# Turnovers between sublayers of a two-layer trunk: sums as 32-column strips partly ahead of the last weight half, low parts of h on GpSimd, and a new order of the first projections

## The reference

```python
def pre_norm(x, mod, j, g):
    return rmsnorm(x, g) * (1 + mod_chunk(mod, 3 * j + 1)) + mod_chunk(mod, 3 * j)

def post_residual(x, out, mod, j, g, w):
    return x + w * mod_chunk(mod, 3 * j + 2) * rmsnorm(out, g)

def swiglu(h, w_in, w_out):
    gate, up = jnp.split(h @ w_in, 2, axis=-1)
    return (jax.nn.silu(gate) * up) @ w_out
```

## Time and profile before

| | |
|---|---|
| median of 3 runs | 1605.79 us (1604.51 to 1605.99) |
| the profiled execution | 1602.07 us |
| its span | 1600.1 us |
| busy, share of the span | PE 96%, DVE 68%, ACT 43%, POOL 3% |
| chain that ended last | PE 81%, DVE 10%, ACT 3% |
| TensorE clock granted | full over the whole span |
| data moved | 259.77 MB, mean 162 GB/s |

### The profile page before, as it was taken

One profiled execution on the slowest core, in us unless ns is written; L12 is line 12 of the kernel. 1 busy time (PEld: TensorE's weight loads), 2 busy tenths in 40 slices (PEclk: granted clock), 3 DMA queues, 4 the chain that ended last, 5 costly groups with the idle time before them and its releaser, 6 DMA issues.

```text
span 1600.1 us, 26085 instructions
## 1 busy us (share of the span) xinstructions
PE 1541.0 (96%) x10631; PEld 1505.8 (94%) x10631; DVE 1085.4 (68%) x1975; ACT 691.0 (43%) x1204; POOL 50.3 (3%) x50
## 2 busy tenths in 40 slices
PE   4999999999889899999999999999999999999999
PEld 4999999989778889999999999999999989999999
DVE  5678889773579797878946778785562885344332
ACT  4433334464566474333434533334463265333333
POOL 2000000002102000000000000000000000000000
PEclk9999999999999999999999999999999999999999
DMA  9765656577321264564545555655454354443311
GB/s 325 249 201 168 200 181 223 184 223 213 89 92 56 66 211 158 185 206 160 197 157 184 167 193 184 197 176 173 133 192 132 106 176 141 131 132 124 102 64 39
DMA packets 255654, 259.77 MB, mean 162 GB/s; under 512 B 6625, under 2 KB 253842, under 8 KB 255538
## 3 DMA queue, kind: packets, MB, share of 16 engines
q1 hardware_dynamic: 250528, 253.25, 48.8%
q10 hardware_dynamic: 4114, 2.84, 0.6%
q0 software_dynamic: 896, 2.06, 0.5%
HBM read 255.50 MB, written 2.62 MB: 161 GB/s over the span
## 4 chain that ended last, share of the span: by engine, by line
PE 81%; DVE 10%; ACT 3%; issue 3%; POOL 1%; DMA 1%; ACTq 0%; DVEq 0%; POOLq 0%
PE bank L444 24%; PE bank L446 24%; PE bank L445 24%; DVE PARTS L1112 1%; DVE WL L413 1%; ACT WH L399 1%; PE bank L466 1%; PE bank L1638 1%; PE bank L468 1%; PE bank L467 1%; DVE X L1178 1%; DVE HL L1141 1%; DVE SUMS L1443 1%; POOL WL L413 1%; DMA MIX<-in_x_sample 1%
## 5 line engine op out<-in xcount | busy, mean ns | idle before, releaser
L413 DVE TENSOR_TENSOR WL<-RAW,WH 128x1024 fp32r<-128x1024 f32 (+1 forms) x335 | 398.6, 1195 | 418.5 <-ACT WH L399 417.7
L399 ACT ACTIVATE WH<-RAW 128x1024 fp32r<-128x1024 f32 (+1 forms) x344 | 357.5, 1043 | 605.3 <-PE bank L446 593.1
L444 PE MATMUL bank<-HH,WH 128*128 128x384 f32 x1664 | 564.2, 339 | 8.0 <-DVE WL L413 3.5
L446 PE MATMUL bank<-HH,WL 128*128 128x384 f32 x1664 | 560.6, 337 | 0.0
L445 PE MATMUL bank<-HL,WH 128*128 128x384 f32 x1664 | 560.4, 337 | 0.0
L444 PEld LDWEIGHTS bank<-HH,WH 128*128 128x128 f32 x1664 | 313.8, 189 | 10.0 <-issue 4.0
L445 PEld LDWEIGHTS bank<-HL,WH 128*128 128x128 f32 x1664 | 313.8, 189 | 0.0
L446 PEld LDWEIGHTS bank<-HH,WL 128*128 128x128 f32 x1664 | 313.7, 189 | 0.0
L444 PE MATMUL bank<-AH,WH 128*128 128x384 f32 x704 | 237.0, 337 | 0.0
L445 PE MATMUL bank<-AL,WH 128*128 128x384 f32 x704 | 236.6, 336 | 0.0
L446 PE MATMUL bank<-AH,WL 128*128 128x384 f32 x704 | 236.6, 336 | 0.0
(11 more groups left out here) (249 smaller groups left out, 1457.2 us busy)
## 6 DMA issues: line engine op xcount, KB each, us to landing
RAW<-in_ffn_w_in SPq DMA_DIRECT2D x88, 1024.0 KB, 5.1
RAW<-in_mod_w SPq DMA_DIRECT2D x72, 1024.0 KB, 5.1
RAW<-in_ffn_w_out SPq DMA_DIRECT2D x32, 1024.0 KB, 5.1
RAW<-in_ab_w_in SPq DMA_DIRECT2D x16, 1024.0 KB, 6.1
RAW<-in_ffn_w_out SPq DMA_DIRECT2D x16, 768.0 KB, 4.6
RAW<-in_cv_w_in SPq DMA_DIRECT2D x12, 1024.0 KB, 5.2
RAW<-in_ab_w_out SPq DMA_DIRECT2D x4, 1024.0 KB, 5.2
RAW<-in_cv_w_out SPq DMA_DIRECT2D x4, 1024.0 KB, 5.2
```

The lines of the kernel that those rows point to most:

```text
L399: e.activation(WH[:, (2 * m + b) % 4, 0:nk, :], RAW[:, p, 0:nk, b * P:(b + 1) * P], ACT.Copy).then_inc(half_hi, 1)
L413: e.tensor_tensor(WL[:, k, 0:nk, :], RAW[:, p, 0:nk, b * P:(b + 1) * P], WH[:, k, 0:nk, :].bitcast(F32), ALU.subtract).then_inc(half_ready, 1)
L444: e.matmul(out, WH[:, k, kk, :], xh(kk), start=(first and kk == 0), stop=False)
L446: mm = e.matmul(out, WL[:, k, kk, :], xh(kk), start=False, stop=(last and kk == nk - 1))
```

## The change

Six edits go together.

1. **Sums as strips.** Each sum matmul of 128 token columns becomes four matmuls of 32 columns, each into its own 32 partitions of the bank. `SUM_COLS` goes from 44 to 16.
2. **Part of the sums ahead.** The sums of the tiles 0 to 5 run ahead of the last output weight half (`early_sums`). Tiles 6 and 7 are no longer added to them by DVE but enter as sums of their own with weights `W67`. DVE's adds go from 24 to 20 a turnover and ACT squares one tile less.
3. **Operands in PSUM.** The small steps of DVE keep `q` in bank 2, `scale_y` writes into bank 3 (tile 0) or bank 7 and waits for all eight scaled tiles from tile 1 on. `spread` uses transposes in place of matmuls.
4. **h.** `HL` of tiles 1 to 7 is made by GpSimd (`low_parts`). The full copy of tiles 3, 5 and 7 is made by DVE, of the others by ACT. DVE makes the sample columns of `HH` of tile 0 itself.
5. **`pe_four`** does both products with `HH` of a tile for all four banks first and then the ones with `HL`; its tail is two tiles long from sublayer 1 on.
6. **Filler steps** are dealt out anew, and ACT does the root ahead of a weight split.

The core of the diff:

```diff
-SUM_COLS = 44
+SUM_COLS = 16
+FULL_DVE = (3, 5, 7)
...
-            high_ready(order[0])
...
-            for kk in order[1:len(order) - tail]:
-                ready(kk)
-                for b in range(4):
-                    e.matmul(outs[b], WH[:, kh[b], kk, :], HH[:, kk, :], start=False, stop=False)
-                    e.matmul(outs[b], WH[:, kh[b], kk, :], HL[:, kk, :], start=False, stop=False)
-                    e.matmul(outs[b], WL[:, kh[b], kk, :], HH[:, kk, :], start=False, stop=False)
-                yield
+            for kk in order[:len(order) - tail]:
+                first = kk == order[0]
+                high_ready(kk)
+                for b in range(4):
+                    if first:
+                        e.wait_ge(half_hi, H + b + 1)
+                    e.matmul(outs[b], WH[:, kh[b], kk, :], HH[:, kk, :], start=first, stop=False)
+                for b in range(4):
+                    if first:
+                        e.wait_ge(half_ready, H + b + 1)
+                    e.matmul(outs[b], WL[:, kh[b], kk, :], HH[:, kk, :], start=False, stop=False)
+                if first:
+                    yield
+                ready(kk)
+                for b in range(4):
+                    e.matmul(outs[b], WH[:, kh[b], kk, :], HL[:, kk, :], start=False, stop=False)
+                yield
...
+            def low_parts(s):
+
+                for d in range(1, KD):
+                    pool.wait_ge(*full_done(s, d))
+                    pool.wait_ge(h_hi, 8 * s + d + 1)
+                    pool.wait_ge(h_ready, 8 * s + d)
+                    pool.tensor_tensor(HL[:, d, :], TT[:, 2 + d % 2, :], HH[:, d, :].bitcast(F32),
+                                       ALU.subtract).then_inc(h_ready, 1)
...
                 root(sum_out(bank[0], 0), 0, (stat_done, 2 * s + 1))
+                nxt[1]()
+                root(STAT[:, 4, :], 5, (sum_step, 5 * (s + 1)))
                 act.wait_ge(xy_done, 8 * s + 8)
                 tile_scaled(s, OUT, 7)
-                root(STAT[:, 4, :], 5, (sum_step, 5 * (s + 1)))
...
-                dve.tensor_tensor(OUT[:, d, :], OUT[:, d, :], cols3(bank[4]), ALU.mult).then_inc(y_scaled, 1)
+                dve.tensor_tensor(scaled_y(OUT, d), OUT[:, d, :], cols3(bank[4]), ALU.mult).then_inc(y_scaled, 1)
...
-                full(s, 0)
+                dve.wait_ge(h_scaled, 8 * s + 1)
+                dve.tensor_scalar(HH[:, 0, SEQ:NT], TT[:, 0, SEQ:NT], CA[:, s, 0, 1:2], MOD[:, 24 * s, 1:2],
+                                  ALU.mult, ALU.add).then_inc(h_hi_sample, 1)
...
-                    low(s, d - 1)
                     if d == 1:
+                        low(s, 0)
+                    if d in FULL_DVE:
                         full(s, d)
-                low(s, KD - 1)
...
-                    mm = pe.matmul(B[:, columns(t)], src[:, t * P:(t + 1) * P], weights(t),
-                                   start=opens and t == 0, stop=closes and t == TOKS - 1)
+                    for strip in range(4):
+                        at = 32 * strip
+                        mm = pe.matmul(B[at:at + 32, columns(t)], src[:, t * P + at:t * P + at + 32], weights(t),
+                                       start=opens and t == 0, stop=closes and t == TOKS - 1)
...
+            def early_sums(s):
+
+                pe.wait_ge(sq_added, 5 * s + 5)
+                sums(bank[0], ACC, one, lambda t: sum_at(t, 0), opens=True)
+                pe.wait_ge(y_added, 5 * s + 5)
+                sums(bank[0], RSTD, one, lambda t: sum_at(t, 1))
+                pe.wait_ge(xy_added, 5 * s + 5)
+                sums(bank[1], ROOT, one, lambda t: sum_at(t, 0), opens=True)
...
+                            if j == 11 and b == 1 and s in SUMMED:
+                                early_sums(s)
...
+                        if d == 7:
+                            early_sums(s)
                         pe_half(pe, f"out{s}", d, hh, hl, 8, cols3(bank[4 + d % 4]), True, True)
```

More of the change, by code:

```diff
@@ L416, in split_dve, with full_done @@
             return out
+        def full_done(s, d):
+            if s == 0:
+                return h_full_dve, d + 1
+            if d in FULL_DVE:
+                return h_full_dve, KD + len(FULL_DVE) * (s - 1) + FULL_DVE.index(d) + 1
+            rest = [k for k in range(KD) if k not in FULL_DVE]
+            return h_full_act, len(rest) * (s - 1) + rest.index(d) + 1
         def out_nk(st, n):
@@ L647, in _ @@
                 half_low(f"in{s}")
+                low_parts(s)
         @block.scalar
```

139 lines of the change are left out of this document (74 added, 65 removed).

## The result

The changed kernel takes 1616.11 us (median of 4 runs, 1612.41 to 1616.84), the kernel before 1605.15 (4 runs beside them): a ratio of 1.0066, interval [1.0051, 1.0082]. It is slower, and outside the forecast range. The profiled execution took 1616.84 us, span 1615.0, mean granted clock of TensorE 0.986; before it was 0.996 and a span of 1600.1. So the clock wasn't full over the whole span before the change either, as the table ahead has it: it stood at 1.2 GHz in the opening (about 24 to 30 us) and for 3.4 us each at 426 and 463 us. Nor is that profile a typical execution: over the 72 executions of the kernel before that ran beside the experiments the mean granted clock runs from 0.990 to 0.996 (median 0.993) and the time from 1600.28 to 1607.42 us, and only ten of them reach 0.995.

What follows compares the result with a forecast made beforehand. TensorE, busy 96% of the span, was taken as the bound. SwiGLU turnovers -5.1, sublayers 1 and 4 +1.5 and last turnover -0.4 sum to -4.0 us: 1601.8 against the median of 1605.79, range 1593.5 to 1608.

Steps and rivals of the forecast that it cites:

- The strip's price: Sums in the turnovers: a unit of four strip matmuls costs 0.09 us, where a full matmul costs 0.236.
- rival 3: Strips load one after another, a unit at 0.236 us; 1615.4 us; chance 0.06.
- The wait of sublayers 1 and 4: Ahead of their last output tile, TensorE waits for DVE's adds of tile 5, idle for 4.1 us.
- T' to the first wide matmul: SwiGLU turnovers: last tile's end, delayed 0.97 us by early sums, to first wide matmul with h: 6.39 us.
- Last turnover: End of the kernel: strips let the root start at 1592.35, not at 1592.78; 0.4 us off.
- GpSimd's low part: h stage: one low part of a tile made by GpSimd takes 0.95 us.
- the last tile ends 4.54 later: Sublayers 1 and 4: waiting for DVE's adds delays the last tile's end 4.54 us; turnovers lose 0.76 and 0.75.
- First wide to next: ... waits 1.7, sum 19.54: From first wide matmul with h to the first projection behind the first four: 19.54 us, waits 1.7 included.
- three `full` of 0.6: h stage: DVE's full copies of tiles 3, 5, 7 take 0.6 us each; last `scaled` 14.5 after the first.
- rival 2: GpSimd becomes the bound of h, DVE and GpSimd holding each other up; 1614.3 us at low parts of 2.0; chance 0.13.
- the opening: Start of the kernel: keeps a tail of one and its wait for GpSimd's four weight halves; no gain.
- Rival 4: Turnovers not shortened, only the idle 1.2 and 0.8 behind the first four gained; 1605.3 us; chance 0.18.

Runs made afterwards that it cites:

- the fastest kernel: Changed kernel with a tail of one; in sublayers 1 and 4 three filler steps, then early sums as whole matmuls, behind the last tile: 1599.06 us, 0.9963.
- three runs: Changed kernel, early sums of sublayers 1 and 4 behind last tile: alone 1614.43 us; with tail of one and filler ahead 1605.51 or behind 1604.63.

## Why the prediction was wrong

**What held.** The strip's price: 72 records of the early sums take 0.80 us, 0.09 a unit, as taken; here the row was right and rival 3 fell. (By the rule of the Trainium skill that the prediction weighed, "TensorE: Matmul & The Clock Gate", section "LDWEIGHTS (loading the stationary operand)", the unit would have stayed at 0.236; the measurement decides against it.) The spread: 0.54 us for three transposes, as taken. The wait of sublayers 1 and 4: with no wait the last tile of sublayer 1 would have begun at 570.54, and it began at 575.12, 4.58 later against 4.54 forecast; 3.21 of it was idle, where I had 4.1. (That 575.12 is also near my 575.4 is luck: the stretch ahead of it was 1.1 us longer than in the profile of before, and began 1.4 earlier.) T' to the first wide matmul: 6.39 forecast, 6.41 in sublayer 0 and 6.03 and 6.04 in 1 and 4. No idle stands behind the first four any more, as forecast. Last turnover: 0.36 off, 0.4 forecast. GpSimd's low part: 0.99 to 1.03 us, 0.95 forecast.

**Failed: "the last tile ends 4.54 later" and every other term that counts standing at its own length.** The sum priced idle time at what it lasts, and so had sublayers 1 and 4 lose 0.76 and 0.75; they lost 5.79 and 5.75. Here idle time also brought TensorE from 2.4 to 1.2 GHz, for 3.4 or 6.8 us: the last tile started 4.58 later and ended 7.3 later. That was readable before: it lost 6.8 us of clock in all, with a fall in the opening, and I didn't ask where new idle of 4 us would leave the clock. The wait alone on the kernel before gives 10.4 us in the medians, where standing alone accounts for 7.2 (twice 4.04, less the 0.44 that each turnover gives back) and the clock behind the two waits for 5.1 in its profile; dummy work in the same wait gives back 5.5.

**Failed: "First wide to next: ... waits 1.7, sum 19.54".** It is 21.28, 21.10 and 21.11 where the clock held (sublayers 0, 1, 4). Beside 16.66 for the matmuls, 0.57 for filler and 0.36 for the modulation transpose, 3.7 remain in sublayer 0, where the sum had 1.9. Of these, 2.06 are named waits, where I had 1.7, and 1.6 are pauses of up to 0.2 us at each halt and each change between groups of matmuls, where I had 0.2; the kernel before has 0.9 of them. The waits go back to "three `full` of 0.6": each pair takes 1.43 to 1.48 beside GpSimd, and the last `scaled` comes 15.53 behind the first, not 14.5. That is rival 2's mechanism, in `full` rather than in the low parts. In exchange for the 1.22 us behind the first four, the tail of two waits 1.14 for the high part of tile 7 and 0.63 for its low part, and behind those the clock fell in two of five turnovers. A tail of one gives 21.09 to 20.43 without a fall there: the second tile held back is worth nothing in the first turnover (0.2) and costs 0.7 to 2.2 in the others. I had seen the 0.65 for the high part and had not seen that the tail makes it longer.

**Left out: that many small instructions in one go stall.** A strip costs 0.011 us a record, but there are four matmuls for one. The changed kernel itself has the stall in sublayer 2:

```profile
871.80 0.33 PE L1679 MATMUL bank<-W,SQ 128*32 128x32 f32 x14 [1.10 <-issue]
```

and one of 0.86 in sublayer 3. With them T to first wide is 7.43 and 7.28 us there and 6.41 in sublayer 0 (0.23 of "issue"). Neither the kernel before nor the one with strips in their old place shows one.

**Left out: the opening.** I gave it nothing; it gained 1.26. The new `pe_four` alone gains 0.96 there, strips and transposes alone 0.41. With the high products first, TensorE has eight matmuls of a tile to do before it asks for the low part; that this is where the 0.96 comes from isn't shown.

**The sum again.** Forecast -4.0 for the span. Take the clock's 15.4 off the measured 14.9, and -0.5 is left; in the medians, 8.4 off 11.0, +2.6 is left. With their 1.7 of clock off, the stretches to next of sublayers 0, 2 and 3 gained 0.1 and lost 1.0 and 0.7. Rival 4 had the turnovers no shorter, but with 1.0 gained in each of these, so it comes nearest and is still too good. Rival 2's 1614.3 comes near the measured time by accident: its mechanism is seen (1.46 us for the pair), but taking the low parts away from GpSimd doesn't make the kernel faster.

**What stays open.** The mixers of sublayers 1 and 4 together lose 3.4 to 6.8 us more of clock than in either profile of before, between 416 and 505 us and at about 1270, in all variants, even in the one that only adds a wait. Nothing there is edited, and the record speaks for this being no effect of the edits. The waits at which the clock falls stand in the kernel before too (2.16 us at 417, 2.39 at 448, 1.67 at 498 and this one), only that in its two profiles the clock fell behind few of them:

```profile
1267.21 0.41 PE L457 MATMUL bank<-HH,WH 128*128 128x384 f32 x1 [2.99 <-issue]
```

And both profiles are of rare executions, with a granted clock of 0.996, where 62 of the 72 beside the experiments have 0.990 to 0.994. What decides in an execution whether the clock falls at such a wait, the runs don't tell. Nor do they tell why the stall of the small matmuls is milder in the SwiGLU turnovers, where the early 72 lie 24 wide matmuls ahead.

## What to carry to other kernels

Price idle time of TensorE ahead of dense work at its length and at the clock behind it: look in the windows for what the granted clock did behind the idle times that exist, and put work that has to be done anyway into a wait that can't be avoided. Before comparing two profiles, look how the granted clock spreads over the unprofiled executions: here the two profiles of before were 3 and 5 us below the median. Saved work is only saved if the chain that the engine waits for gets shorter too. A small VectorE step in that chain can stand behind a long GpSimd operation; its row is then ten times as long as its neighbours. When a matmul is split into strips, count instructions as well as time, and look for idle put down to "issue" in the middle of a group: that row tells of a limit that no semaphore shows.

## What the runs showed of the hardware

- TensorE's granted clock went from 2.4 to 1.2 GHz in pieces of 3.4 or 6.8 us (1.7 or 3.4 lost; once, in the opening of the run with dummy work, 10.2 us): behind 2.53 + 0.68 us of idle, behind 4.04, behind 1.14 + 0.64, behind 1.77. Not every time: the same 1.14 + 0.63 in sublayer 0, the 1.77 in sublayer 2 of the run with strips alone, the 2.99 at 1267 us before, and the 1.22 of before had none. In the fastest kernel it fell at 577 us, with no idle ahead of it but three microseconds of small matmuls.
- The 32-column strips of the early sums take 0.011 us a record, so 0.09 a unit of four in two passes (0.80 for nine units), where a whole matmul of 16 moving columns takes 2.18/9 = 0.24.
- After 158 to 174 small records, TensorE stood for 2.1 to 2.8 us with nothing to wait for, until 4.65 to 4.79 us behind the last wide matmul, in both turnovers of sublayers 1 and 4 of three runs; with 138 records in the first 4.0 us (24 of filler and 114 of sums) it did not.
- VectorE's `TENSOR_SCALAR` pair, SBUF to SBUF, took 1.43 to 1.48 us in place of 0.67 while GpSimd ran a 384-column operation; VectorE's products with an operand in PSUM kept their 0.55 to 0.56 beside it.
- A VectorE step of 128x3 with both inputs in SBUF took 1.01 to 1.92 us in the run with strips alone and ended with GpSimd's 1024-column operation in all five turnovers; with its operands in PSUM it took 0.16 or 0.17 beside one.
